# Choosing 128 of 1024 tokens on 32 partitions of 512 values instead of 16 of 1024

## What is computed

```
aff = softmax(h @ w_router)                       # (tokens, 16)
top_aff, top_idx = top_k(aff.T, cap)              # per expert, cap = 2 * tokens / 16
xg = h[top_idx]
y = (silu(xg @ w_gate) * (xg @ w_up)) @ w_down * top_aff
out = zeros.at[top_idx].add(y)
```

## Time and profile before

| what | value |
|---|---|
| median of 3 runs | 4529.52 us (4527.68 to 4533.71) |
| profiled execution, its own time | 4533.75 us |
| its span, first to last instruction | 4532.1 us |
| PE busy | 4215.3 us, 93% of the span |
| DVE busy | 1371.6 us, 30% |
| ScalarE busy | 1019.1 us, 22% |
| chain that ended last: PE | 74% |
| same chain: DVE | 4% |
| mean granted TensorE clock | 0.963 of full |

### The profile page before, as it was taken

How to read it: one execution, slowest core, us unless ns; L and a number is a source line. 1 busy time by engine, 2 the same in 40 slices (tenths; PEclk the granted TensorE clock), 3 DMA queues, 4 the chain that set the end, 5 groups by cost and what they waited for, 6 DMA issues and landing times.

```text
span 4532.1 us, 67015 instructions
## 1 busy us (share of the span) xinstructions
PE 4215.3 (93%) x26176; PEld 3042.1 (67%) x26176; DVE 1371.6 (30%) x3314; ACT 1019.1 (22%) x2364; POOL 198.6 (4%) x228
## 2 busy tenths in 40 slices
PE   7999999999999399999997999999999966999995
PEld 4556667655545399999996555667544435999995
DVE  1326666301034611111112445566210253111113
ACT  1226555200012011111111324555200110000001
POOL 0000000000000000000000000000000000000002
PEclk9999999999999599999998999999999987999997
DMA  6120000422245578888885221000212435999994
GB/s 199 46 74 27 15 15 8 123 81 71 70 141 195 185 233 263 261 261 261 261 252 160 77 74 44 15 15 8 80 42 65 135 111 171 317 309 317 312 315 159
DMA packets 577538, 653.26 MB, mean 144 GB/s; under 512 B 36260, under 2 KB 510980, under 8 KB 577368
## 3 DMA queue, kind: packets, MB, share of 16 engines
q1 hardware_dynamic: 563064, 605.77, 41.8%
q0 software_dynamic: 14304, 45.10, 4.0%
HBM read 579.95 MB, written 70.86 MB: 144 GB/s over the span
## 4 chain that ended last, share of the span: by engine, by line
PE 74%; issue 11%; DVE 4%; DMA 1%; ACT 1%; DVEq 0%; POOL 0%; POOLq 0%; SPq 0%; ACTq 0%
PE PS L632 47%; PE PS L636 6%; PE PS L925 6%; PE PS L791 6%; PE PS L849 3%; PE PS L842 2%; PE PS L769 1%; PE PS L1058 1%; DVE arena L1659 1%; DVE arena L1661 1%; DVE arena L1665 1%; DVE arena L1339 1%; PE PS L647 1%; PE PS L855 1%; PE PS L776 0%
## 5 line engine op out<-in xcount | busy, mean ns | idle before, releaser
L632 PE MATMUL PS<-arena 128*128 128x128 f32 (+6 forms) x13760 | 2775.3, 363 | 21.0 <-DMA arena<-in_w_in 5.5
L632 PEld LDWEIGHTS PS<-arena 128*128 128x128 f32 x13760 | 2054.5, 192 | 722.4 <-issue 614.0
L1339 DVE TENSOR_TENSOR arena<-arena,PS 128x160 f32<-128x160 f32 (+3 forms) x336 | 125.1, 382 | 1629.4 <-ACT arena L1319 939.1
L636 PEld LDWEIGHTS PS<-arena 128*128 128x128 f32 (+1 forms) x3082 | 372.7, 142 | 323.5 <-issue 222.7
L636 PE MATMUL PS<-arena 128*128 128x128 f32 (+1 forms) x3082 | 472.5, 280 | 73.1 <-DVE arena L1339 38.5
L1319 ACT ACTIVATE arena<-PS 128x160 f32<-128x160 f32 (+1 forms) x256 | 74.3, 290 | 1371.7 <-PE PS L632 1371.7
L791 PE MATMUL PS<-arena 96*128 96x512 f32 (+1 forms) x800 | 361.9, 535 | 14.8 <-issue 12.8
L925 PE MATMUL PS<-arena 128*128 128x512 f32 x576 | 261.0, 608 | 11.4 <-DVE arena L1339 7.2
L1170 ACT ACTIVATE arena<-PS 128x256 f32<-128x256 f32 (+1 forms) x408 | 198.7, 488 | 256.4 <-PE PS L636 245.1
L1492 DVE TENSOR_REDUCE arena<-PS 128x1 f32<-128x512 f32 (+1 forms) x384 | 231.0, 603 | 76.8 <-PE PS L791 71.5
L1339 DVE TENSOR_TENSOR arena<-PS,arena 128x64 f32<-128x64 f32 (+5 forms) x332 | 113.8, 383 | 322.7 <-PE PS L925 147.7
(11 more groups left out here) (162 smaller groups left out, 1873.1 us busy)
## 6 DMA issues: line engine op xcount, KB each, us to landing
arena<-in_w_exp_gate SPq DMA_DIRECT2D x128, 1024.0 KB, 6.4
arena<-in_w_exp_up SPq DMA_DIRECT2D x128, 1024.0 KB, 8.7
arena<-in_w_exp_down SPq DMA_DIRECT2D x128, 1024.0 KB, 7.2
arena<-in_w_ada SPq DMA_DIRECT2D x24, 2048.0 KB, 16.6
arena<-in_w_in SPq DMA_DIRECT2D x32, 512.0 KB, 5.4
h_transposed<-arena SPq DMA_DIRECT2D x20, 512.0 KB, 4.4
x_mid<-arena SPq DMA_DIRECT2D x18, 512.0 KB, 2.7
moe_sum<-arena SPq DMA_DIRECT2D x18, 512.0 KB, 3.2
```

The source lines that it names most:

```text
L632: m = pe.matmul(o, lt, rh, start=start and i == 0, stop=stop and i == n - 1)
L636: return pe.transpose(o, i, ident)
L1339: return dve.tensor_tensor(o, x, y, op)
```

## The change

The 1024 affinities of an expert are split in two halves of 512 tokens, on partitions 0 to 15 and 16 to 31. 16 rounds run on these 32 partitions with two passes instead of three: the 8 largest, and strike them out. The state after each round is written to another group of 32 partitions (four groups of four states, `snap`), so that all 16 states are kept. At the end four `max_index` over all 128 partitions look up the positions of all rounds, since each state stands where its round's values stand. This gives the sorted best 128 of each half. The best 128 of both together are the larger of the r-th of the one half and the (127 - r)-th of the other: PE brings values and indices to columns (`candidates`, eight matmuls), ScalarE copies them (`cand`), PE multiplies the second half by a reversing matrix (`reversed_half`, two matmuls), and DVE compares and picks (six instructions).

Also: PE transposes two 16-wide tiles at once (4 instead of 8 transposes for the latent tokens; DVE writes the affinities in that order, in two instructions where l = 0); chunk 8 moves behind these transposes; the context rounds run behind the latent ones with a `topk` and a PE function of their own (`context`); a small Exp on ScalarE is put between `logits_a(TT - 2)` and `tr_a(TT - 1)`; `rev` is built by a copy of the identity with its columns reversed; the matmul for `modT` writes to another PSUM bank. The diff's core:

```diff
+                pe.wait_ge(*s("aff", 1))
+                if l == 0:
+                    for t in range(TC):
+                        tr(PS[0:E, 3, t * P:(t + 1) * P], affp[:, t, :])
+                for i in range(4):
+                    m = tr(PS[0:32, 7, i * P:(i + 1) * P], affp[:, TC + 2 * i:TC + 2 * i + 2, :])
+                m.then_inc(s["affT"], 1)
+                if l == 0:
                     pe.wait_ge(G["rowc"], 8 + 7)
                     ada_chunk(8, 1, 1, 6)
...
+                def candidates():
+                    pe.wait_ge(*s("topk", 1))
+                    for i, v in enumerate((vals, idxf)):
+                        for q in range(4):
+                            m = pe.matmul(PS[q * 32:(q + 1) * 32, 2, i * 32:(i + 1) * 32], v, ident[:, q * 32:(q + 1) * 32], start=True, stop=True)
+                    m.then_inc(s["sel"], 1)
+                def reversed_half():
+                    pe.wait_ge(*s("sel_up", 1))
+                    pe.matmul(PS[:, 4, 0:E], rev, cand[:, E:2 * E], start=True, stop=True)
+                    pe.matmul(PS[:, 4, E:2 * E], rev, cand[:, 3 * E:4 * E], start=True, stop=True).then_inc(s["sel"], 1)
...
                 logits_a(TT - 2)
+                A(stat[:, 25:26], epsc[:, 0:1], ACT.Exp)
                 tr_a(TT - 1)
...
                 act.wait_ge(*s("sel", 1))
+                A(cand, PS[:, 2, 0:64], ACT.Copy).then_inc(s["sel_up"], 1)
...
+                dve.tensor_copy(snap[0:32, 0, :], PS[0:32, 7, :])
+                if l == 0:
+                    dve.tensor_copy(ctxr[0:E, 0, :], PS[0:E, 3, 0:CTX])
                 dve.drain()
+                for r in range(16):
+                    i, q = r // 4, slice(r % 4 * 32, r % 4 * 32 + 32)
+                    o8 = vals[q, i * 8:(i + 1) * 8]
+                    dve.max(o8, snap[q, i, :])
+                    dve.drain()
+                    if r < 15:
+                        q2 = slice((r + 1) % 4 * 32, (r + 1) % 4 * 32 + 32)
+                        dve.match_replace(snap[q2, (r + 1) // 4, :], o8, snap[q, i, :], -1.0)
+                        dve.drain()
+                for i in range(4):
+                    dve.max_index(idx8[:, i * 8:(i + 1) * 8], vals[:, i * 8:(i + 1) * 8], snap[:, i, :])
+                dve.drain()
+                dve.tensor_copy(idxf, idx8).then_inc(s["topk"], 1)
...
+                dve.wait_ge(*s("sel", 2))
+                va_, ia_, vb_, ib_ = cand[:, 0:E], cand[:, 2 * E:3 * E], PS[:, 4, 0:E], PS[:, 4, E:2 * E]
+                TTR(pick[:, 0, :], va_, vb_, ALU.is_ge)
+                dve.scalar_tensor_tensor(out=pick[:, 1, :], in0=ia_, scalar=-512.0, in1=ib_, op0=ALU.add, op1=ALU.subtract)
+                TTR(affS[:, 0, :], va_, vb_, ALU.max)
+                dve.drain()
+                TTR(pick[:, 2, :], pick[:, 1, :], pick[:, 0, :], ALU.mult)
+                dve.drain()
+                m = dve.scalar_tensor_tensor(out=idxT[:, 0, :], in0=pick[:, 2, :], scalar=float(CTX + 512), in1=ib_, op0=ALU.add, op1=ALU.add)
```

More of the change, by code:

```diff
@@ L73, in layer_counts @@
     n |= {k: 2 * tiles for k in "x1T mst".split()}
-    n |= {k: 1 for k in "sm_m sm_e aff affT topk sel sel_cp".split()}
+    n |= {k: 1 for k in "sm_m sm_e aff affT sel_up sel_cp".split()}
+    n |= dict(topk=2, sel=3)
     n |= {k: E for k in "stage_g stage_s xa xd".split()}
@@ L193, in build @@
         afft = at(O + 22816, TT, E)
[L195 to L199, removed]
+        affp = at(O + 22656, TT, E)
+        snap = at(O + 23040, 4, 512)
+        vals = at(O + 25344, 32)
+        idx8 = at(O + 25376, 32).bitcast(U32)
+        idxf = at(O + 25408, 32)
+        cand = at(O + 25440, 64)
+        rev = at(O + 25504, P)
+        pick = at(O + 25632, 3, E)
+        ctxr = at(O + 7168, 2, CTX)
         valc = at(O + 25728, CAP_C)
@@ L982, in _ @@
                     pe.wait_ge(G["modT_cp"], 1)
[L985 to L1000, removed]
                     pe.wait_ge(*s("y_used", NT[l]))
@@ L1006, in _, with context @@
                     pe.wait_ge(G["rowc"], 8 + 12)
-                select()
+                def candidates():
[8 more added lines that the diff above has]
+                    pe.matmul(PS[:, 4, E:2 * E], rev, cand[:, 3 * E:4 * E], start=True, stop=True).then_inc(s["sel"], 1)
+                def context():
+                    pe.wait_ge(*s("topk", 2))
+                    pe.matmul(PS[0:CAP_C, 3, 2 * E:3 * E], idcf[0:E, :], ident[0:E, 0:E], start=True, stop=True)
+                    pe.matmul(PS[:, 3, 3 * E:4 * E], four[0:E, 0].rearrange("p j c -> p (j c)"), ident[0:E, 0:E], start=True, stop=True)
+                    pe.matmul(PS[:, 3, 4 * E:5 * E], four[0:E, 1].rearrange("p j c -> p (j c)"), ident[0:E, 0:E], start=True, stop=True).then_inc(s["sel"], 1)
+                candidates()
+                reversed_half()
                 if l == 0:
+                    context()
                     pe.wait_ge(G["modr_in"], 32 + 16)
-                    pe.matmul(PS[:, 3, 0:96], mrow[0:96, :], ident[0:96, 0:96], start=True, stop=True).then_inc(G["modT"], 1)
+                    pe.matmul(PS[:, 7, 0:96], mrow[0:96, :], ident[0:96, 0:96], start=True, stop=True).then_inc(G["modT"], 1)
                 N = NN[l]
@@ L1636, in _ @@
                 nt = NT[l]
+                dve.tensor_copy(rev, ident[:, ::-1])
                 dve.wait_ge(*s("rt_cp", nt))
@@ L1649, in _ @@
                 dve.wait_ge(*s("affT", 1))
-                dve.tensor_copy(affT[0:E, tl * P:TOK], PS[0:E, 5:8, :].rearrange("p b n -> p (b n)")[:, tl * P:TOK])
+                dve.tensor_copy(snap[0:32, 0, :], PS[0:32, 7, :])
+                if l == 0:
+                    dve.tensor_copy(ctxr[0:E, 0, :], PS[0:E, 3, 0:CTX])
                 dve.drain()
[L1653 to L1658, removed]
+                for r in range(16):
[7 more added lines that the diff above has]
+                        dve.drain()
@@ L1659, in _ @@
+                for i in range(4):
+                    dve.max_index(idx8[:, i * 8:(i + 1) * 8], vals[:, i * 8:(i + 1) * 8], snap[:, i, :])
+                dve.drain()
+                dve.tensor_copy(idxf, idx8).then_inc(s["topk"], 1)
+                if l == 0:
+                    for r in range(4):
+                        cur, o8 = ctxr[0:E, r % 2, :], valc[0:E, r * 8:(r + 1) * 8]
                         dve.max(o8, cur)
                         dve.drain()
-                        dve.max_index(ii[0:E, r * 8:(r + 1) * 8], o8, cur)
@@ L1662, in _ @@
[L1662 to L1667, removed]
+                        dve.max_index(idc8[0:E, r * 8:(r + 1) * 8], o8, cur)
+                        if r < 3:
+                            dve.match_replace(ctxr[0:E, 1 - r % 2, :], o8, cur, -1.0)
+                        dve.drain()
@@ L1668, in _ @@
+                    dve.tensor_copy(idcf[0:E, :], idc8[0:E, :])
                     dve.drain()
-                    dve.tensor_scalar(ff[0:E, :], ii[0:E, :], float(base), None, ALU.add)
-                    dve.drain()
-                if l == 0:
                     for i, v in enumerate((valc, idcf)):
                         dve.tensor_copy(four[0:E, i], v[0:E, :].unsqueeze(1).to_broadcast([E, 4, CAP_C]))
-                dve.drain().then_inc(s["topk"], 1)
-                dve.wait_ge(*s("sel", 1))
@@ L1676, in _ @@
-                dve.tensor_copy(idxT[:, 0, :], PS[:, 2, 0:E])
-                m = dve.tensor_copy(affS[:, 0, :], PS[:, 2, E:2 * E])
+                    dve.drain().then_inc(s["topk"], 1)
+                dve.wait_ge(*s("sel", 2))
+                va_, ia_, vb_, ib_ = cand[:, 0:E], cand[:, 2 * E:3 * E], PS[:, 4, 0:E], PS[:, 4, E:2 * E]
+                TTR(pick[:, 0, :], va_, vb_, ALU.is_ge)
+                dve.scalar_tensor_tensor(out=pick[:, 1, :], in0=ia_, scalar=-512.0, in1=ib_, op0=ALU.add, op1=ALU.subtract)
@@ L1678, in _ @@
+                TTR(affS[:, 0, :], va_, vb_, ALU.max)
+                dve.drain()
+                TTR(pick[:, 2, :], pick[:, 1, :], pick[:, 0, :], ALU.mult)
+                dve.drain()
+                m = dve.scalar_tensor_tensor(out=idxT[:, 0, :], in0=pick[:, 2, :], scalar=float(CTX + 512), in1=ib_, op0=ALU.add, op1=ALU.add)
                 if l == 0:
-                    dve.tensor_copy(idxT[0:CAP_C, 1, :], PS[0:CAP_C, 2, 2 * E:3 * E])
-                    dve.tensor_copy(affC, PS[:, 2, 3 * E:4 * E])
+                    dve.wait_ge(*s("sel", 3))
+                    dve.tensor_copy(idxT[0:CAP_C, 1, :], PS[0:CAP_C, 3, 2 * E:3 * E])
+                    dve.tensor_copy(affC, PS[:, 3, 3 * E:4 * E])
@@ L1683, in _ @@
                     dve.drain()
-                    m = dve.tensor_scalar(idxC, PS[:, 2, 4 * E:5 * E], 4.0, colb[:, 0:1], ALU.mult, ALU.add)
+                    m = dve.tensor_scalar(idxC, PS[:, 3, 4 * E:5 * E], 4.0, colb[:, 0:1], ALU.mult, ALU.add)
                 m.then_inc(s["sel_cp"], 1)
```

7 lines of the change are left out of this document (5 added, 2 removed).

## The result

The changed kernel takes 4466.27 us (median of 4 runs, 4465.37 to 4468.66) against 4530.77 for the kernel before in the same comparison: a ratio of 0.9857, 95% interval 0.9844 to 0.9870, 64.5 us less. The forecast was 4461.9, 67.6 us less, with most of it between 4454 and 4470. The two profiled executions differ by 65.1 us in span (4532.1 and 4467.0).

The account below looks back on a forecast made before the run. DVE's choice of tokens, 60.5 us in layer 1 and 66.6 in layer 0, was taken as paid in full. Savings of 31.2 and 36.4 us, 67.6 together, from 4529.5 gave 4461.9; most between 4454 and 4470, range to 4473.

Parts of the forecast that it names:

- The rounds and look-ups: Choice of tokens on DVE, first MAX8 to PE: 27.3 us in place of 60.5, 33.2 us less in each layer.
- partitions cost no time: DVE passes: time depends on values per row, 1.04 ns each, and not on the number of partitions.
- The rival of the slow strike-out: MATCH_REPLACE8 across partition groups runs at a fraction of its rate; at an eighth, 111 us more, time 4573; chance 0.03.
- an estimate of 2.1 us in all: MATCH_REPLACE8 held 0.07 us behind its load, 15 times in two layers; total then 4464.0.
- In front, layer 1: Before the first MAX8: Exp loses 0.9, four transposes save 0.85, shorter copy saves 0.53; sum 0.5 us earlier.
- Behind, layer 1: From PE's start on the candidates to the staging copy: 3.9 us, 2.5 more than before; ends 1.7 to 4.2 more.
- Layer 0 to the staging: Layer 0's stage of indices done at 1521.2 instead of 1560.20, 39.0 us earlier, candidates and merge hidden beside context rounds.
- POOL's start: Layer 0, POOL's issue behind the staging left at 3.17 us; possibly 2.2 less or some 4 more.
- The landing under load: Layer 0's gathers fall into full queues and take 7.5 us instead of 4.85, 2.65 us lost.
- The first rival: Layer 0's gathers served behind the weight blocks, landing about 1544, not 1533.2: 10.8 us, 4472.7; chance 0.13.
- the weights end at 1538.5: Layer 0's weight blocks, 9 MB at 348 GB/s, run until about 1538.5 instead of 1537; PE does not wait.
- The clock, expected neutral: Behind both gathers, PE's granted clock starts at half and returns to full as before: neither gain nor loss.

Follow-up runs that it names:

- e2: Changed kernel with halving alone: look-up in every round again, states in two buffers on the same 32 partitions; 4479.67 us.
- e6: Changed kernel without the small Exp on ScalarE; 4461.59 us.
- the yardstick: The changed kernel run once more, unaltered, as comparison for the other runs on the same chip; 4464.59 us.
- e3: Changed kernel with SP holding weight blocks 6 to 11 of layer 0's first expert until both gathers have landed; 4459.50 us.
- e4: Changed kernel with one context round, then merge and staging of the latent indices, then the other context rounds in layer 0; 4459.47 us.
- e8: Changed kernel with one small load issued by POOL and waited for before its first gather; 4459.67 us.
- e1: Changed kernel with the small Exp moved behind `tr_a(TT - 1)`; 4459.98 us.
- e9: e7 with e8's small early POOL load added; 4450.31 us, ratio 0.9818 to the kernel before.
- e5: e4 with weight blocks held from c = 4 and the small Exp behind `tr_a`; 4454.65 us.
- e7: e5 with 40 extra PE transposes in front of PE's wait for the first gather of each layer; 4451.62 us.

## Why the prediction came out

**The rounds and look-ups, 33.2 us a layer: right, 0.7 too much.** A round is 1.603 us where I had 1.56; from the first MAX8 to the conversion 27.7 us where I had 27.0. (Of the round that I took the gaps from, the strike-out is 0.41 us long with 0.07 behind it, where I wrote 0.40 and 0.08; the sum is the same.) The load of the match values takes 79 ns behind a drained MAX8, and the 59 of the old loop only behind a FIND_INDEX8 (e2 shows both); MATCH_REPLACE8 from group to group takes 13 ns more than within one, FIND_INDEX8 on 128 partitions 13 ns more than on 32, so "partitions cost no time" was right only to that. The rival of the slow strike-out is out. Of the Trainium skill, page "VectorE: DVE Perf Modes", section "Two Vector instructions with no wait between them", I had made an estimate of 2.1 us in all: the pause between load and MATCH_REPLACE8 that it asks for is there in the changed kernel and not in e2, but it is about 15 ns and not 70, with the 13 of the longer pass some 0.8 us in all. The Trainium skill's page "Vector Engine (DVE) Microarchitecture Reference", section 3.8, which calls such moves free, is right here but for the 13 ns.

**In front, layer 1: the step failed in its size.** I took the chain through `tr_a` alone, ScalarE's half of the last router input. DVE's half, `tr_d`, ended 0.7 us behind it before, so half of the delay was covered. Booked 0.9 for the Exp, measured 0.1 (e6); the sum in front 1.3 us earlier, not 0.5. In layer 0 the same Exp costs 1.3 us by the yardstick's trace and 0.9 by the first one of the changed kernel, where I had 1.5.

**Behind, layer 1: 2.77 us, not 3.9.** The eight matmuls with 32 columns took 0.50 us to ScalarE's start where I took 1.5, below my lower end (0.9 and 0.2), so that the relay costs 1.4 and not 2.5 more. That is also below the 1.7 at which I put the lower end of the whole relay; the two ends that I gave for the matmuls carry only from 2.1 to 3.0, and the rest of my 1.7 to 4.2 has no working. With 0.7 too much for the rounds, 0.8 too little in front, 1.1 too little here and 0.1 behind the staging, layer 1 gave 32.6 us to the rows where I had 31.2.

**Layer 0 to the staging: 39.2 against 39.0, in part by luck.** The order of things was right: the candidates and the merge hidden beside the context rounds, chunks 9 to 11 done before the candidates (the last copy at 1510.5, the candidates at 1513.7). But two misses cancel in the sum. The first MAX8 came 5.6 us earlier and not 4.6, most of it because the clock was at full at the six transposes of the affinities (0.82 us, where I had booked 1.44). From there to the staging it took 36.5 us and not 35.7: the rounds, and 0.2 in the context rounds.

**POOL's start: left at 3.2 us, was 6.4.** I had named the cause, code that comes through full queues, and put it into the range (some 4 more) and not into the sum. This is the largest term missed, 3.3 us. e3, e4 and e8 bear the cause out; what the 2 us between the packet and the gather are stays open.

**The landing under load: PE had the rows 6.8 us behind the context gather's issue, the landing alone was booked at 7.5.** The first rival, gathers served behind the weights, is out: PE took the rows up at 1536.9, and DMA stayed full until about 1548 (share 1.08 from 1544 to 1548, 0.07 in the next 4 us). I had the weights end at 1538.5, 10 us too early, which touched no step of the chain. With POOL's start and the landing, layer 0 gave 34.1 us to the rows where I had 36.4.

**The clock, expected neutral: 1.6 us lost in this execution.** The first eighth of the first expert took 6.26 and 5.97 us before, 7.47 and 6.32 after, while every later one is 4.35 and 3.57. But over the eleven traces that have the change in them (the changed kernel twice, e1 to e9) it is 5.99 to 7.67 in layer 0 and, without the extra transposes, 5.23 to 6.35 in layer 1; the second look at the same changed kernel has 7.65 and 5.24. It depends on when the granted clock rises after the expert has begun: in the changed kernel the expert began at 1542.25 and the clock was still 0.50 up to 1548; in e3, with 6.17 us, it began at 1533.3 and the clock was 0.94 from 1536 to 1540. In layer 1 the 5.97 of before lies within what the same later code shows, so there this is scatter. In layer 0 eight of the eleven lie above the 6.26 of before, of which there is one trace; a cost of the change there, of up to about a microsecond, is neither shown nor excluded.

Together: 66.7 us to the rows against 67.6, and 65.2 with the clock. The mechanism was as forecast, but that the sum came within 1 us is luck in part: 1.4 too little in layer 1 and 2.3 too much in layer 0 nearly cancel.

## What to carry to other kernels

Here POOL, coming to its first gather, waited for a packet of instructions that came through the same DMA engines as the weights. Where an engine starts late behind its release and the trace shows such a packet in the gap, let that engine run one small instruction of the same stretch early (e8, 4.9 us), or hold the bulk loads back for a few microseconds (e3, 5.1 us). Before costing an operation that is put in front of another, look up which of the engines that feed the next step is last today: the delay counts only beyond that one. A search that repeats over rows pays by the row's length and hardly by the partitions (13 ns of 686 from 32 to 128), so splitting a row over twice the partitions and merging at the end costs a relay of 2.8 us (1.4 more than before) and saves nearly half of every pass (684 ns instead of 1217).

## What the runs showed of the hardware

POOL's first gather stood 6.4 to 6.5 us behind its release with DMA full (six traces), 3.2 to 3.6 with it idle or running empty (four kernels: a share of 0.01 in the kernel before, 0.41 in e3, 0.25 in e5 and 0.34 in e7), and 0.8 to 1.0 in layer 1 and behind the early load of e8 and e9. In the first ten cases a packet of 8 KB on the instruction queue stands in the gap, 4.1 to 4.2 us behind the release with DMA full and 1.1 to 1.3 otherwise, and the gather comes 2.0 to 2.3 us behind it. The two packets of the changed kernel's gap were 0.7% of DMA's time in it; by these places what costs is not their size but the wait for one of them.

A MATCH_REPLACE8 over 32 partitions that reads one group of 32 and writes the next took 677 ns, 13 more than in e2 within one group, and started some 15 ns behind the end of its load, where in e2 there is no pause.

Forty transposes of no use, given to PE while it waited, brought the granted clock to full (1.00 instead of 0.50) before the first expert of layer 1 and took 2.7 us off that stretch (e7 against e5); in layer 0 the clock was back at 0.50 after a pause of 2.7 us behind them.
